# Gated recurrence heads on one core: score terms as full-array products, state terms on arrival, and the next head's scans ahead of the output

## What is computed

```python
def chunked_gated_linear_scan(q, k, v, log_f):          # chunks of 64 tokens
    b = jnp.cumsum(log_f, axis=2)                        # inside a chunk
    b_last = b[:, :, -1]
    b_mid = b[:, :, CHUNK // 2][:, :, None]
    scores = jnp.einsum('bnthd,bnshd->bnhts', q * jnp.exp(b - b_mid), k * jnp.exp(b_mid - b))
    scores = jnp.where(lower_tri, scores, 0.0)
    o_intra = jnp.einsum('bnhts,bnshv->bnthv', scores, v)
    chunk_state = jnp.einsum('bnshd,bnshv->bnhdv', k * jnp.exp(b_last[:, :, None] - b), v)
    def step(S, inp):
        dec, U = inp
        return dec[..., None] * S + U, S
    _, S_in = lax.scan(step, S0, (chunk_decay, chunk_state))   # chunk_decay = exp(b_last)
    o_inter = jnp.einsum('bnthd,bnhdv->bnthv', q * jnp.exp(b), S_in)
    return o_intra + o_inter

o_f = chunked_gated_linear_scan(qp, pad(k_f), vp, pad(lf_f))
o_b = flip(chunked_gated_linear_scan(flip(qp), flip(pad(k_b)), flip(vp), flip(pad(lf_b))))
o = (o_f + o_b)[:, n_pad:]
```

## Time and profile before

| | |
|---|---|
| median of 3 runs | 3708.66 us (3707.41 to 3708.86) |
| profiled execution, its own time | 3714.49 us |
| its span in the profile | 3712.8 us |
| mean granted clock of TensorE | 0.9 of 2.4 GHz |
| PE busy | 3146.8 us, 85% |
| DVE, ACT, POOL busy | 1187.5, 864.8, 793.5 us |
| the stage of the four heads | from 2092.7 to 2228.7 us |

### The profile page before, as it was taken

One profiled execution on the slowest core, in us unless ns is written; L12 is line 12 of the kernel. 1 busy time (PEld: TensorE's weight loads), 2 busy tenths in 40 slices (PEclk: granted clock), 3 DMA queues, 4 the chain that ended last, 5 costly groups with the idle time before them and its releaser, 6 DMA issues. The chain is left out here.

```text
span 3712.8 us, 47030 instructions
## 1 busy us (share of the span) xinstructions
PE 3146.8 (85%) x19302; PEld 2060.4 (55%) x19302; DVE 1187.5 (32%) x1922; ACT 864.8 (23%) x1193; POOL 793.5 (21%) x325
## 2 busy tenths in 40 slices
PE   6997866999989998899988768898688888888885
PEld 3774755787767855688768647344433333333332
DVE  3524435767173033422232246442310111111102
ACT  2325344223132233322323333110100000000001
POOL 1321102333424312333423103000011111111110
PEclk9998778999999998999989868889799999999998
DMA  6326002455322221223321102103199999999996
GB/s 217 87 63 210 3 2 91 147 181 164 85 74 91 91 57 46 68 90 98 102 68 57 58 2 67 48 1 124 72 410 409 423 415 406 407 411 405 408 403 241
DMA packets 245914, 631.19 MB, mean 170 GB/s; under 512 B 18661, under 2 KB 191750, under 8 KB 220753
## 3 DMA queue, kind: packets, MB, share of 16 engines
q1 hardware_dynamic: 234961, 618.68, 44.4%
q0 software_dynamic: 10240, 8.43, 0.7%
q10 hardware_dynamic: 576, 2.10, 0.1%
HBM read 633.33 MB, written 20.97 MB: 176 GB/s over the span
## 5 line engine op out<-in xcount | busy, mean ns | idle before, releaser
L502 PE MATMUL ps<-arena_parts,arena_parts 128*128 128x512 f32 (+1 forms) x2080 | 782.0, 376 | 103.1 <-POOL ring_parts L386 33.0
L504 PE MATMUL ps<-arena_parts,ring_parts 128*128 128x512 f32 (+1 forms) x2080 | 773.3, 372 | 0.0
L386 POOL TENSOR_TENSOR ring_parts<-ring,arena_parts 128x2048 fp32r<-128x2048 f32 (+1 forms) x104 | 507.3, 4879 | 1089.4 <-ACT arena_parts L380 1089.4
L3317 PE MATMUL ps<-arena 128*64 128x512 f32 x1024 | 516.2, 663 | 163.0 <-DMA arena<-in_w_up 103.5
L503 PE MATMUL ps<-hT_parts,arena_parts 128*128 128x512 f32 (+1 forms) x1728 | 630.4, 365 | 0.0
L3318 PE MATMUL ps<-arena 128*64 128x512 f32 x1024 | 517.7, 664 | 0.0
L502 PEld LDWEIGHTS ps<-arena_parts,arena_parts 128*128 128x128 f32 x2080 | 397.9, 191 | 194.3 <-issue 67.1
L504 PEld LDWEIGHTS ps<-arena_parts,ring_parts 128*128 128x128 f32 x2080 | 397.7, 191 | 71.3
L3317 PEld LDWEIGHTS ps<-arena 128*64 128x64 f32 x1024 | 150.0, 152 | 497.5 <-issue 495.6
L503 PEld LDWEIGHTS ps<-hT_parts,arena_parts 128*128 128x128 f32 x1728 | 329.9, 191 | 51.7
L380 ACT ACTIVATE arena_parts<-ring 128x2048 fp32r<-128x2048 f32 (+1 forms) x105 | 210.6, 2007 | 391.4 <-PE ps L504 346.3
(11 more groups left out here) (503 smaller groups left out, 3780.6 us busy)
## 6 DMA issues: line engine op xcount, KB each, us to landing
arena<-in_w_gate SPq DMA_DIRECT2D x64, 2048.0 KB
arena<-in_w_up SPq DMA_DIRECT2D x64, 2048.0 KB, 22.6
arena<-in_w_down SPq DMA_DIRECT2D x64, 2048.0 KB, 22.6
ring<-in_ffn_up SPq DMA_DIRECT2D x44, 1024.0 KB, 5.1
arena<-in_ada_w SPq DMA_DIRECT2D x20, 2048.0 KB, 9.9
ring<-in_ret_w_in SPq DMA_DIRECT2D x24, 1024.0 KB, 5.3
ring<-in_ffn_down SPq DMA_DIRECT2D x16, 1408.0 KB, 7.1
ring<-in_gdn_w_in SPq DMA_DIRECT2D x16, 1024.0 KB, 5.7
```

Source lines behind the costliest of these rows:

```text
L386: pool.tensor_tensor(self.lower(n, kt, cols), self.slot(n, kt, cols), self.upper(room, n, kt, cols), ALU.subtract)\
L502: pe.matmul(out, upper[:, r], self.upper[r][:, part], start=(r == 0), stop=False)
L504: ins = pe.matmul(out, lower[:, r], self.upper[r][:, part], start=False, stop=(r == self.tiles - 1))
L3317: pe.matmul(k.ps[upper, 2 + u, :], m.xeT[u][:, r, :], m.w_up[u][:, r, :], start=(r == 0), stop=(r == KD - 1))
```

## The change

`A` is moved to another buffer (`spare`) and made twice as wide: for each pair of chunks 128 by 128, with each chunk's scores in its block of the diagonal and zeros in the other two blocks. The output of a head lies in bank 7 alone. PE first waits for the copy of the output of the head before and writes zeros over the bank with one product of 512 columns, weights `zeros`, which opens the accumulation; then it adds the terms of scores, one product of full weights for each pair and direction (8), and then the terms of states, 8 forward and 7 backward, each with a wait for its own state. None of these goes through `by_columns`. ACT copies the output with one instruction.

DVE signals `scaled` behind `qs`; both products into `qe` come behind it, after a wait (from the second head on) until PE has signalled the output `o` of the head before. The wait for `o_copied` at DVE's head is gone. ACT takes the exponentials of the next head (`powers(i + 1)`) between its copy of the scores and its copy of the output. POOL copies the next `v` when PE has transposed the last one and POOL's own masks are done. DVE's and ACT's loops are written out.

```diff
--- before.py
+++ after.py
@@ -2411,9 +2411,10 @@
         self.b, self.qs, self.ks, self.kd = two(L2), two(T), two(T), two(L2)
         self.vtok = room.take(self.PAIRS + 1, P)
         self.kdtok = two(self.PAIRS + 1, P)
-        self.A = two(self.PAIRS, CH)
+        self.A = [k.spare[:, d * T:(d + 1) * T].rearrange("p (n c) -> p n c", c=P) for d in range(2)]
         self.S = two(NCH, P)
         self.qe = two(T)
+        self.zeros = room.take(P)
         self.dec = two(NCH + 1)
 
     def tile(self, n, i):
@@ -2446,13 +2447,11 @@
         k, g = self.k, self.g
         k.wait_tables(dve, "meta")
         meta = slice(0, N_META)
-        with dve.Fori(0, HYT) as i:
-            st.enter(i, 2)
+        for i in range(HYT):
             for d in range(2):
 
-                logf = g.logf[:, bass.ds(i + d * HYT, 1), :].rearrange("p o t -> p (o t)")
+                logf = g.logf[:, i + d * HYT, :]
                 runs = g.runs[:, d, :]
-                self.wait(dve, "o_copied", i + 1)
                 if d == 0:
                     ins = dve.tensor_tensor_scan(self.b[d], runs, logf, 0.0, ALU.mult, ALU.add)
                 else:
@@ -2476,8 +2475,11 @@
                 else:
                     dve.tensor_tensor(self.kd[d][:, N_META:], self.kd[d][:, N_META:], kk[:, N_META:], ALU.mult)
                 dve.tensor_tensor(self.ks[d], self.ks[d], kk[:, N_META:], ALU.mult)
-                dve.tensor_tensor(self.qs[d], self.qs[d], q, ALU.mult)
-                dve.tensor_tensor(self.qe[d], self.b[d][:, N_META:], q, ALU.mult).then_inc(self.sem("scaled"), 1)
+                dve.tensor_tensor(self.qs[d], self.qs[d], q, ALU.mult).then_inc(self.sem("scaled"), 1)
+            if i:
+                self.wait(dve, "o", i)
+            for d in range(2):
+                dve.tensor_tensor(self.qe[d], self.b[d][:, N_META:], self.tile(0, i)[:, N_META:], ALU.mult)
             for d in range(2):
 
                 order = self.ORDER[d]
@@ -2495,11 +2497,11 @@
                     passed = order[n - 1] if d == 0 else order[n]
                     dec = self.dec[d][:, passed:passed + 1]
                     dve.scalar_tensor_tensor(self.S[d][:, n, :], self.S[d][:, n - 1, :], dec, add, ALU.mult, ALU.add).then_inc(self.sem("state"), 1)
-            st.leave(HYT)
 
     def scalar(self, act):
         k = self.k
-        with act.Fori(0, HYT) as i:
+
+        def powers(i):
             for d in range(2):
                 self.wait(act, "diff", i * 2 + (d + 1))
                 last = CH - 1 if d == 0 else 0
@@ -2513,6 +2515,8 @@
                 self.wait(act, "e", i * 4 + (2 * d + 2))
                 act.activation(self.dec[d][:, 0:NCH].unsqueeze(2), self.chunks(self.b[d])[:, :, last:last + 1], ACT.Copy).then_inc(self.sem("exp"), 1)
 
+        powers(0)
+        for i in range(HYT):
             self.wait(act, "turned", i * 3 + 1)
             act.activation(self.vtok[:, 0:self.PAIRS], k.ps[:, 0, :].rearrange("p (n c) -> p n c", c=P), ACT.Copy)
             act.activation(self.vtok[0:N_META, self.PAIRS], k.ps[0:N_META, 1, 0:P], ACT.Copy).then_inc(self.sem("tok"), 1)
@@ -2526,28 +2530,30 @@
                 self.wait(act, "scored", i * 2 + (d + 1))
                 scores = k.ps[:, 4 + d, 0:self.PAIRS * CH].rearrange("p (n c) -> p n c", c=CH)
                 for row, _, first, end in self.quarters(d):
-                    rows = slice(row, row + CH // 2)
-                    ins = act.activation(self.A[d][rows, :, first:end], scores[rows, :, first:end], ACT.Copy)
+                    rows, at = slice(row, row + CH // 2), row // CH * CH
+                    ins = act.activation(self.A[d][rows, :, at + first:at + end], scores[rows, :, first:end], ACT.Copy)
                 ins.then_inc(self.sem("A"), 1)
+            if i < HYT - 1:
+                powers(i + 1)
             self.wait(act, "o", i + 1)
-            pairs = lambda ap: ap.rearrange("p (n c t) -> p c n t", c=2, t=CH)
-            for half, bank in enumerate((7, 5)):
-                ins = act.activation(pairs(self.tile(0, i)[:, 0:T])[:, half], pairs(k.ps[:, bank, :])[:, half], ACT.Copy)
-            ins.then_inc(self.sem("o_copied"), 1)
+            act.activation(self.tile(0, i)[:, 0:T], k.ps[:, 7, :], ACT.Copy).then_inc(self.sem("o_copied"), 1)
 
     def gpsimd(self, pool):
+        pool.memset(self.zeros, 0.0)
         for d in range(2):
             pool.memset(self.A[d], 0.0)
         pool.sem_inc(self.sem("o_copied"), 1)
         for i in range(HYT):
-            self.wait(pool, "o_copied", i + 1)
+            if i:
+                self.wait(pool, "turned", i * 3 - 2)
+                self.wait(pool, "masked", i * 2)
             pool.tensor_copy(self.vT, self.tile(3 * HYT, i)).then_inc(self.sem("v"), 1)
             for d in range(2):
 
                 self.wait(pool, "A", i * 2 + (d + 1))
                 sign = 1 if d == 0 else -1
                 for half in range(2):
-                    part = self.A[d][half * CH:(half + 1) * CH]
+                    part = self.A[d][half * CH:(half + 1) * CH, :, half * CH:(half + 1) * CH]
                     ins = pool.affine_select(out=part, in_=part, compare_op=ALU.is_ge, fill=0.0, base=0,
                                              pattern=[[0, self.PAIRS], [sign, CH]], channel_multiplier=-sign)
                 ins.then_inc(self.sem("masked"), 1)
@@ -2588,20 +2594,20 @@
                         ins = mm(self.added(d, n), self.kdtok[d][rows, c // 2], self.vtok[rows, c // 2], start=True, stop=True)
                 ins.then_inc(self.sem("u"), 1)
 
+            self.wait(pe, "o_copied", i + 1)
+            pe.matmul(k.ps[:, 7, :].rearrange("p (n c) -> p n c", c=P), self.zeros, k.ident[:].unsqueeze(1).to_broadcast([P, self.PAIRS, P]), start=True, stop=False)
             self.wait(pe, "masked", i * 2 + 2)
-            self.wait(pe, "state", i * (2 * NCH - 3) + (2 * NCH - 3))
+            out = lambda c: k.ps[:, 7, c * CH:(c + 1) * CH]
+            for d in range(2):
+                for n in range(self.PAIRS):
+                    pe.matmul(k.ps[:, 7, n * P:(n + 1) * P], self.vtok[:, n], self.A[d][:, n], start=False, stop=False)
             for c in range(NCH):
-                rows = slice((c % 2) * CH, (c % 2 + 1) * CH)
-                at = slice(c * CH, (c + 1) * CH)
-                terms = []
-                for d in range(2):
-                    terms.append((self.vtok[rows, c // 2], self.A[d][rows, c // 2]))
-                    n = c if d == 0 else NCH - 2 - c
-                    if n >= 0:
-                        terms.append((self.S[d][:, n, :], self.qe[d][:, at]))
-                for n, (lhsT, rhs) in enumerate(terms):
-
-                    ins = mm(k.ps[:, (7, 5)[c % 2], at], lhsT, rhs, start=(n == 0), stop=(n == len(terms) - 1))
+                self.wait(pe, "state", i * (2 * NCH - 3) + max(c, 1))
+                pe.matmul(out(c), self.S[0][:, c, :], self.qe[0][:, c * CH:(c + 1) * CH], start=False, stop=False)
+            for n in range(NCH - 1):
+                c = NCH - 2 - n
+                self.wait(pe, "state", i * (2 * NCH - 3) + NCH - 1 + max(n, 1))
+                ins = pe.matmul(out(c), self.S[1][:, n, :], self.qe[1][:, c * CH:(c + 1) * CH], start=False, stop=(n == NCH - 2))
             ins.then_inc(self.sem("o"), 1)
```

## The result

The changed kernel takes 3659.31 us, median of 4 runs (3648.66 to 3664.86), the kernel before 3708.76 beside it (3707.41 to 3710.17): a ratio of 0.9863, interval 0.9840 to 0.9886, 49.4 us less. The forecast was 3657.5 in a range of 3649 to 3668.

A forecast was written before the change was run, and what follows sets the result against it. No engine was full: a chain from engine to engine bound the four-head stage. Its 135.7 us would lose 51.9, less 1 for code and waits: 3663.5 by the profile, 3657.7 by the median, forecast 3657.5, range 3649 to 3668.

The forecast's parts named there:

- Head turn: Between heads: scans no longer wait for the output copy; 20.97 us of the 33.64 us period remain; unrolled code costs nothing.
- Output: PE's output products: zeros 0.87 us, then 8 of scores and 15 of states at 0.23 each, at full clock.
- the tail of the last head: Behind the last backward state: output ends 2.0 us after it instead of 11.7.
- Head 1: First head of the stage: as before to its last state, 21.69 - 0.86 = 20.83 us, so ending at 2113.5.
- Period: From one head's first scan to the next: 20.11 us instead of 33.64.
- the step of 0.86 for `qe`: Products into `qe` behind the `scaled` signals: first `kd` turn 0.61 us earlier, 0.86 in all per head.
- Sum: Whole stage: head 1, three periods of 20.11 and the tail end at 2176.7; saving 51.9 us, 51 after taking 1 off.
- A: Rival: output at clock 0.50, tail 7.8 us, each of three turns loses 1.5; saving 40.6, time 3668; chance 0.22 with mixtures.
- B: Rival: next head still waits for the output, only the output gets shorter; 22.9 us a head, time 3667; chance 0.05.
- C: Rival: loads and passes of output products do not overlap, 1.30 us each; stage 34 longer, time 3743; chance 0.02.
- D: Rival: a hidden wait (POOL's masks, the bank's zeros) puts the old period back; time 3709; chance 0.01.
- Stages behind: Stages after the heads: the forecast falls if they change length by more than 2 us.

The follow-up runs named there:

- `x3_columns`: Changed kernel with its 8 products of scores and 15 of states issued in four column groups each: 3656.85 us in one run, 3653.44 us timed in rounds.
- the first two experiments: Changed kernel with the old hand-over between heads, 3667.82 us; new order of DVE, ACT and POOL with the old output, 3683.44 us.
- the grouped kernel: Kernel before, with zeros written over both output banks, then the old 31 terms with all 64-row ones before the 128-row ones: 3680.28 us, single run.
- control: Kernel before, with the same zeros over both output banks, then the 31 terms in their old order: 3706.06 us, single run.
- the first experiment: Changed kernel, but DVE waits for the copied output before a head's scans and ACT copies it before the next exponentials: 3667.82 us.

## Why the prediction held, point by point

- *Head turn.* Right. DVE idles nowhere between heads; undoing it cost 8.5 us.
- *Output.* Scores and states at 0.23 a product and full clock, as priced; from the zeros' start to the first product of scores it is 0.96 in head 2, for 0.87; the tail of the last head is 1.8 (2177.07 to 2178.90) for 2.0. The full clock was the right choice, but the prediction's reason, products that fill the array, is only in part shown: issued in column groups (`x3_columns`) the output kept the full clock as well. What a product would cost at half clock, 0.46 or less, stays open, since no head of the changed kernel has its output there.
- *Head 1.* Missed by 1.9: its last state ends at 2115.40, not 2113.5. DVE waits 2.80 for ACT, where it had waited 1.57. ACT's table load of 1.28, which ran beside DVE's scans (at 2092.82), now stands behind the wait for `diff`. It does so in the kernels of the first two experiments as well, which have ACT's loop written out; in the grouped kernel and its control, which keep the loop, it runs beside the scans as before. The prediction had put the unrolled code at nothing, with 0 and 1 us as its bounds; that was too tight, since what unrolling moved was this load. It is 1.2 of the 1.9. The rest is 0.9 for the second `kd` turn and the scores and 0.26 for `qe`, both as in the next point, less 0.5 because PE's additions take 1.6 here for 2.1.

```profile
2096.90 1.28 ACT L2509 ACT_TABLE_LOAD   x1 [4.26 <-DVE arena L2469]
```

- *Period.* 20.56 on average for 20.11. The second `kd` turn was taken over at the old head's 1.35, but the clock rises later now and it takes 1.94, the scores 1.32 for 0.99; that loses 0.9. The first scan, no longer beside POOL's copy, gives 0.38 back. And the step of 0.86 for `qe` was too large: 0.6 was measured, since the first `qe` product had filled a wait of 0.57 for ACT's second exponentials. What remains is 0.1 less of waiting for ACT's first ones (1.47 for 1.57) and 0.1 by which the next scan's record starts before the last state's ends.
- *Sum.* 2.9 us short in the stage: 1.9 for head 1, 3 x 0.45 for the periods, 0.3 back in the tail. 48.9 us saved in the stage for 51.9 forecast, of which 1 had been taken off. That the time came within 1.8 us of the forecast is partly luck: terms of the sum missed in both directions, and the changed kernel's own runs spread over 16 us.
- *Rivals.* A is out, the output's clock was 1.00. B is out: DVE does not wait between heads; built as the first experiment, it gave 3667.8 for 3667. C is out: records of a product start 0.12 apart, not 0.65. D is out: no wait put the old period back.
- *Stages behind.* The prediction had staked itself on their keeping their length within 2 us. From the output copy to the end of the span they were 6.4 us shorter in the first profile. Most of that is the mixer, whose length differs as much between two profiles of the kernel before. So the prediction's own condition failed, by a scatter that it had no term for, and this is why the profiled spans differ by 55.6 us and the medians by 49.4.

## What to carry to other kernels

When small products alternate between 64-row and 128-row tiles, look first at whether they can be grouped by size behind one product that opens the bank; here that alone took some 20 us off the stage, by one profile of each order, and whole products were not needed for it. A tail and an overlap that hides it must not be counted as two gains. After such a change read what waits in the new order: here a wait of 3.3 us in DVE's program had room for the next head's scans, which took 5 to 6 us off the stage.

## What was not expected of the hardware

- The granted clock fell from 1.00 to 0.50 after 1.75 us of alternating terms, PE busy 10.60 of 10.60 us, and likewise within 3.1 us in the control's other heads; through the same terms grouped it stayed at 1.00 in three heads of four.
- At full clock 31 float32 terms of 64 columns took 3.39 us grouped by tile size, 0.11 each, and 0.25 each where 64-row and 128-row tiles alternated.
- A float32 term with 128 columns of weights and 64 moving columns takes 0.23 us in one piece and 0.11 in four column groups at full clock; with 128 moving columns both take 0.23.
- A stage that is not touched and has the same records took 172.0 to 179.3 us, following its granted clock of 0.93 to 0.88, within one kernel too (179.3 and 173.7). Profiles are to be compared stage by stage.
